# Feed-forwards fed with the unnormalised stream, and one convolution tile moved to TensorE, in a float32 four-layer model

## What is computed

```python
def rms_norm(x, g):
    y = x * lax.rsqrt(jnp.mean(x * x, axis=-1, keepdims=True) + EPS)
    return y * g
def swiglu(x, w_gate, w_up, w_down):
    return (jax.nn.silu(x @ w_gate) * (x @ w_up)) @ w_down

h = h + 0.5 * swiglu(rms_norm(h, ffn1_g), wg, wu, wd)     # 1024 -> 2816 -> 1024
h = h + mixer(rms_norm(h, mix_g))                         # even mixer in layer 0, odd mixer in layer 1
h = h + 0.5 * swiglu(rms_norm(h, ffn2_g), wg, wu, wd)
h = h + sigmoid(rms_norm(h, ple_g) @ wgate) * (p @ wproj)

def odd_mixer(xn):                                        # the second mixer
    u, v = split(gelu(xn @ w_in[:, :1024])); v = layer_norm(v)
    c_out = u * (w_s applied to v over blocks of 128 tokens, + c_b_s)
    a, g = split(xn @ w_in[:, 1024:]); hd = a * sigmoid(g)
    hd = causal depthwise convolution of hd, 31 taps, 512 channels, + d_conv_b
    d_out = silu(layer_norm(hd))
    return concat([c_out, d_out]) @ w_out
```

## Time and profile before

| | us |
|---|---|
| runs (3), median | 3446.67 (3442.4 to 3448.03) |
| the profiled execution, device time | 3462.87 |
| its span in the trace | 3461.6 |
| TensorE busy | 3215.9 (93% of the span), mean granted clock 0.95 |
| VectorE busy | 1208.5 (35%) |
| ScalarE busy | 1120.6 (32%) |
| GpSimd busy | 1203.7 (35%) |
| chain that ended last | PE 87%, DVE 8%, issue 1%, ACT 1%, POOL 1%, DMA 1% |

### The profile page before, as it was taken

One profiled execution on the slowest core, in us unless ns is written; L12 is line 12 of the kernel. 1 busy time (PEld: TensorE's weight loads), 2 busy tenths in 40 slices (PEclk: granted clock), 3 DMA queues, 4 the chain that ended last, 5 costly groups with the idle time before them and its releaser, 6 DMA issues.

```text
span 3461.6 us, 36877 instructions
## 1 busy us (share of the span) xinstructions
PE 3215.9 (93%) x14620; PEld 2574.8 (74%) x14620; DVE 1208.5 (35%) x2276; ACT 1120.6 (32%) x1942; POOL 1203.7 (35%) x522
## 2 busy tenths in 40 slices
PE   7999998989999989999839999989999989999998
PEld 5888667767888768887617888768758877877786
DVE  4001485742001430013972111254444233155442
ACT  3222333333223432223203222343222341345422
POOL 3444431014444434444404444443314532300043
PEclk9999998799999999999969999989999999979999
DMA  4333221002333223333202333323213325300032
GB/s 127 96 97 97 82 73 37 1 19 92 95 96 97 84 75 97 98 98 95 91 0 93 96 98 98 91 80 104 91 38 97 98 77 171 105 6 1 13 96 74
DMA packets 76526, 274.51 MB, mean 79 GB/s; under 512 B 8471, under 2 KB 9367, under 8 KB 75972
## 3 DMA queue, kind: packets, MB, share of 16 engines
q1 hardware_dynamic: 76356, 272.16, 25.2%
HBM read 269.98 MB, written 2.15 MB: 79 GB/s over the span
## 4 chain that ended last, share of the span: by engine, by line
PE 87%; DVE 8%; issue 1%; ACT 1%; POOL 1%; DMA 1%; SPq 0%; ACTq 0%; DVEq 0%; POOLq 0%
PE ps L463 24%; PE ps L465 23%; PE ps L464 23%; PE ps L1251 4%; PE ps L1238 4%; PE ps L1228 4%; DVE arena L1848 3%; DVE inv L596 1%; PE ps L2270 1%; DVE arena L642 1%; PE ps L591 1%; POOL arena L582 1%; PE ps L2134 1%; PE ps L1446 1%; ACT w_hi L427 1%
## 5 line engine op out<-in xcount | busy, mean ns | idle before, releaser
L448 POOL TENSOR_TENSOR w_lo<-ring,w_hi 128x1024 fp32r<-128x1024 f32 x473 | 1147.5, 2427 | 2195.2 <-ACT w_hi L427 2195.2
L463 PE MATMUL ps<-x_hi,w_hi 128*128 128x512 f32 x2376 | 945.6, 398 | 49.2 <-DVE x_lo L637 49.2
L464 PE MATMUL ps<-x_lo,w_hi 128*128 128x512 f32 x2376 | 932.3, 392 | 0.0
L465 PE MATMUL ps<-x_hi,w_lo 128*128 128x512 f32 x2376 | 932.2, 392 | 0.0
L427 ACT CAST w_hi<-ring 128x1024 fp32r<-128x1024 f32 x473 | 494.3, 1047 | 947.3 <-PE ps L465 945.5
L463 PEld LDWEIGHTS ps<-x_hi,w_hi 128*128 128x128 f32 x2376 | 451.5, 190 | 152.1 <-issue 59.5
L464 PEld LDWEIGHTS ps<-x_lo,w_hi 128*128 128x128 f32 x2376 | 451.6, 190 | 98.7 <-issue 5.3
L465 PEld LDWEIGHTS ps<-x_hi,w_lo 128*128 128x128 f32 x2376 | 450.7, 190 | 95.6
L463 PE MATMUL ps<-r_hi,w_hi 128*128 128x512 f32 x1088 | 425.7, 391 | 20.7 <-issue 20.7
L464 PE MATMUL ps<-r_lo,w_hi 128*128 128x512 f32 x1088 | 425.3, 391 | 0.0
L465 PE MATMUL ps<-r_hi,w_lo 128*128 128x512 f32 x1088 | 424.9, 391 | 0.0
(11 more groups left out here) (202 smaller groups left out, 2763.6 us busy)
## 6 DMA issues: line engine op xcount, KB each, us to landing
ring<-in_stream SPq DMA_DIRECT2D x473, 512.0 KB, 3.6
arena<-in_cmp_w SPq DMA_DIRECT2D x16, 512.0 KB, 4.6
arena<-frev SPq DMA_DIRECT2D x1, 3072.0 KB, 15.0
h<-in_x SPq DMA_DIRECT2D x4, 512.0 KB, 5.6
out<-arena SPq DMA_DIRECT2D x4, 512.0 KB
arena<-in_p SPq DMA_DIRECT2D x2, 512.0 KB
arena<-in_mem SPq DMA_DIRECT2D x1, 1024.0 KB
arena<-in_pool_recip SPq DMA_DIRECT2D x1, 1024.0 KB
```

The lines of the kernel that those rows point to most:

```text
L448: self.nc.gpsimd.tensor_tensor(self.w_lo[:, n % SPLIT, :], self.ring[:, n % RING, :], self.w_hi[:, n % SPLIT, :].bitcast(F32), ALU.subtrac ...
L463: nc.tensor.matmul(out, a[0], b[0], start=start, stop=False)
L464: nc.tensor.matmul(out, a[0], b[1], start=False, stop=False)
L465: return nc.tensor.matmul(out, a[1], b[0], start=False, stop=stop)
```

## The change

**Feed.** For all four feed-forwards `Normalise` is replaced by `Feed`. Its operands are h times gain, without the norm's factor: ACT rounds (`Feed.round`), DVE makes the rest in one instruction (`Feed.rest`), from `h` itself as soon as a tile of `h` is written. In `Rows` and in the ple's `dense_gated` these steps are woven into the evacuation of the last tiles. The sum of squares moves into the feed-forward: ACT squares (`squares`), DVE adds 7 times (`add`), TensorE sums once (`total`, behind the gate product of tile 1), ACT roots, DVE inverts. The factor is then multiplied in at evacuation: DVE scales the gate product to SBUF, DVE scales the up product to SBUF, ACT applies SiLU, DVE multiplies. So SiLU now waits for DVE. The norms ahead of the two mixers, of ple and of the second block stay.

**Start.** The DMAs are issued as vec, x0, slab 0, x1, slab 1, x2, x3, cst; the small tables become an `Aside` of the first feed-forward, and `Rotary` stands behind its tile 1.

**Second mixer.** Convolution tile 3 goes to TensorE as 31 matmuls with diagonal weights, which ACT makes during the evacuations; DVE gates that tile behind tile 1. The layer norm over the convolution is woven with the normalisation and mixing of v. The output product starts with tile 0, then 4 to 7, then 1 to 3.

```diff
+class Feed:
+    def round(self, act, c):
+        if self.written:
+            act.wait_ge(k.s["h_written"].handle, k.s["h_written"].at(c + 1))
+        k.nc.scalar.activation(k.x_hi[:, c, :], k.h[:, c, :], ACT.Copy,
+                               scale=k.v(self.gain, c)).then_inc(self.rounded.handle, 1)
+    def rest(self, dve, c):
+        dve.wait_ge(self.rounded.handle, self.rounded.at(c + 1))
+        k.nc.vector.scalar_tensor_tensor(k.x_lo[:, c, :], k.h[:, c, :], k.v(self.gain, c), k.x_hi[:, c, :].bitcast(F32),
+                                         ALU.mult, ALU.subtract).then_inc(self.ready.handle, 1)
...
 class Rows:
+        if self.feed:
+            k.high(act, self.first + self.n - 1 + SPLIT)
+            for c in range(KT):
+                self.feed.round(act, c)
...
             self.evacuate(m, k.ps[:, (self.bank + m) % 8, :]).then_inc(self.read.handle, 1)
+            if self.feed and m >= 1:
+                self.feed.rest(dve, m - 1)
...
 def ffn(...):
-            norm.first_two(pe, [k.slab(pe, first + j, P) for j in range(2)], (P, P), (part, done))
+            feed.first_two(pe, [k.slab(pe, first + j, P) for j in range(2)], (part, done))
...
-                        pe.wait_ge(read.handle, read.at(f - 2))
+                        pe.wait_ge(up_scaled.handle, up_scaled.at(f - 2))
...
+                    if f == 1 and j == 0:
+                        feed.total(pe, total_bank)
...
-            norm.act(act)
+            feed.squares(act)
+            k.high(act, first + 3 + SPLIT)
+            feed.sqrt(act, total_bank)
...
-                act.wait_ge(part.handle, part.at(f + 1))
-                nc.scalar.activation(hidden[:, f, :], k.ps[:, 2 * (f % 3), :], ACT.Silu).then_inc(gate.handle, 1)
+                act.wait_ge(gate_scaled.handle, gate_scaled.at(f + 1))
+                nc.scalar.activation(hidden[:, f, :], hidden[:, f, :], ACT.Silu).then_inc(gate.handle, 1)
                 k.high(act, first + 2 * f + 1 + SPLIT)
...
-            norm.dve(dve)
-            if rotary:
-                rotary.dve(dve)
+            feed.add(dve)
+            feed.invert(dve)
...
+                dve.wait_ge(part.handle, part.at(f + 1))
+                nc.vector.tensor_tensor(hidden[:, f, :], k.ps[:, 2 * (f % 3), :], inv, ALU.mult).then_inc(gate_scaled.handle, 1)
+                dve.wait_ge(done.handle, done.at(f + 1))
+                nc.vector.tensor_tensor(up[:, f % 2, :], k.ps[:, 2 * (f % 3) + 1, :], inv,
+                                        ALU.mult).then_inc(up_scaled.handle, 1)
...
+                nc.vector.tensor_tensor(hidden[:, f, :], hidden[:, f, :], up[:, f % 2, :], ALU.mult).then_inc(ready.handle, 1)
+                if rotary and f == 1:
+                    rotary.dve(dve)
...
 def odd_mixer(k):
+            for tap in range(31):
+                ins = nc.tensor.matmul(k.ps[:, conv_bank, :], diag[:, tap, :], g[:, last, tap:tap + SEQ],
+                                       start=(tap == 0), stop=(tap == 30))
```

More of the change, by code:

```diff
@@ L808, in dense_gated @@
     n = len(widths)
-    free = k.s["h_written"] if square else read
+    free = k.s["h_written"] if square or feed else read
     k.slabs_end(done, [done.at(m + 1) for m in range(n)])
@@ L866, in _ @@
                         rows.rest(dve, i)
+                if feed and m == n - 1:
+                    for c in range(2):
+                        feed.rest(dve, c)
                 dve.wait_ge(gate.handle, gate.at(m + 1))
                 ins = finish(m, buf[0:w, m % 4, :])
-                ins.then_inc((k.s["h_written"] if square else read).handle, 1)
+                ins.then_inc(free.handle, 1)
+            if feed:
+                for c in range(2, KT):
+                    feed.rest(dve, c)
             if square:
@@ L876, in dense_gated @@
             k.bank_read[m % 8] = gate.token(m + 1)
-    for g in (done, gate) + (() if square else (read,)):
+    for g in (done, gate) + (() if square else (free,)):
         g.advance(n)
@@ L952, in dve @@
             self.square.dve(dve)
-        else:
+        elif self.feed:
+            self.feed.rest(dve, KT - 1)
+        if not self.square:
             self.read.advance(KT)
@@ L1163, in _, with ple @@
             down.dve(dve, 5)
-    norm.close()
+    feed.close()
     if projection:
         projection.close()
-    for g in (part, done, gate, read):
+    for g in (part, done, gate, ready, gate_scaled, up_scaled):
         g.advance(FT)
-def ple(k, layer, projection):
+def ple(k, layer, projection, feed=None):
     nc = k.nc
@@ L1855, in last_tiles @@
[L1855 to L1865 removed]
+            gate(c)
@@ new lines, in _ @@
+            for c in range(4):
+                act.wait_ge(centred.handle, centred.at(c + 1))
+                nc.scalar.activation(sq[:, c, :], o[:, 4 + c, :], ACT.Square).then_inc(squared.handle, 1)
+            act.wait_ge(sums.handle, sums.at(4))
+            nc.scalar.activation(root, k.ps[:, square_bank, :], ACT.Sqrt, bias=k.c("eps"),
+                                 scale=1.0 / 512).then_inc(lrooted.handle, 1)
+            act.wait_ge(mix_done.handle, mix_done.at(1))
+            rows.round(act, 0)
@@ L1935, with tile_ready @@
+    def tile_ready(act, i):
+        if OD_ROWS[i] < 4:
+            act.wait_ge(mix_done.handle, mix_done.at(OD_ROWS[i] + 1))
+        else:
+            act.wait_ge(s["conv_silu"].handle, OD_ROWS[i] - 3)
+    rows.alone(tile_ready, begun=1)
+    mix_done.advance(4)
+    return feed
 MEM_KV = (10240, 8192)
```

413 lines of the change are left out of this document (278 added, 135 removed).

## The result

| | before | after |
|---|---|---|
| median of the runs, us | 3447.35 (3442.4 to 3455.49, 4 runs) | 3374.03 (3361.68 to 3375.78, 4 runs) |
| the profiled execution: time, span | 3462.87, 3461.6 | 3361.68, 3359.6 |
| TensorE busy | 3215.9 (93%) | 3188.5 (95%) |
| VectorE busy | 1208.5 (35%) | 1314.3 (39%) |

The ratio is 0.9771 (95% interval 0.975 to 0.9792), 73.3 us less. The forecast was 3373. Single executions are read here by stretches of their traces, not by their times: the runs come from several chips, and on one of them a run of before took 3455.32.

What follows compares the result with a forecast made beforehand. TensorE, busy 93%, was taken to bound the kernel, so gains come only where it stands still or runs slowly. Terms 11.8 + 11.5 + 10.6 + 3.9 + 35.8 = 73.6 us, off the median 3446.7: 3373.1; range 3359 to 3395.

Steps and rivals of the forecast that it cites:

- Second mixer: Last value matmul to output product: starts 34.5 us earlier, about 1.3 more from the slow clock; 35.8 gained.
- Odd handover: Layer 1, mixer to feed-forward: 14.2 us of gap and slow clock go, 2.4 lost again; 11.8 gained.
- Even handover: Layer 0, mixer to feed-forward: 13.9 us of gap and slow clock go, 2.4 lost again; 11.5 gained.
- ple: Handover from ple to feed-forward: a 4.6 us wait stays; 11.5 gained less 0.9 for the sum, 10.6.
- Start: First feed-forward: 13.8 us gained, less 0.9, 2.2 for other products, 4.8 waiting behind angle tables, 2.0 in clock; 3.9.
- rival 1: First feed-forward: no wait behind the angle tables, a further 6.8 us less, giving 3366; chance 0.15.
- The other tiles: Feed-forward tile loops: SiLU may be 7.1 us late, scaling makes it 1.3 late; costed at nothing.
- The rule against one term: Mixer handovers: DVE's two-operand instructions hold POOL too, delaying splits; each would gain 0.7 us less, sum 72.2.
- 2: Second mixer: TensorE keeps 1.2 GHz through the taps, which take 52.7 us; 3394; chance 0.08.
- 3: Handovers keep gaps of 3 to 6 us and the clock falls: 4 less each, 16 in all; 3389; chance 0.11.
- 4: Tile loops: DVE's chain makes TensorE wait once per tile, 88 times; at 1 us 3461; chance 0.03.
- 5: TensorE waits for a bank or ACT at each start, so only the mixer's tail gains; 3411; chance 0.03.

Runs made afterwards that it cites:

- mixer_only: The kernel before with only the new second (odd) mixer, feed-forwards still normalised by `Normalise`; 3419.13 us, ratio 0.9917.
- gate_early: The changed kernel with the gate of tile 3 ahead of tile 1's taps on DVE instead of behind them; 3378.28 us in one run.
- feed_only: The changed kernel with the old second mixer and plain output row order, still fed into the changed feed-forward; 3412.58 us, ratio 0.9896.
- after_again: The changed kernel run again unaltered, in more rounds; 3374.07 us, ratio 0.9786.
- rotary_split: The changed kernel with the angle tables' DVE work in two pieces, behind tiles 3 and 4, ACT's part behind tile 6; 3369.23 us, one run.
- loop_probe: The changed kernel with two more unused reciprocals per tile on DVE, from the fifth tile on, in all four feed-forwards; 3377.62 us, one run.
- rotary_tile9: The changed kernel with the angle tables whole but behind tile 9, ACT's part at tile 11; 3363.94 us, one run.
- best_taps8: The changed kernel with the three edits, the last tile's gate early and 8 of tile 2's taps moved to TensorE; 3364.36 us, ratio 0.9761.
- three edits: The changed kernel with angle tables in two pieces, tile 1 applied before the scalings, ACT's rounding before the cast at ple; together 3369.47 us, ratio 0.9773.
- ple_round_first: The changed kernel with ACT rounding the first two tiles behind ple before casting the next weight slab; 3361.74 us in one run.

## Why the prediction was right, point by point

- **Second mixer.** Predicted 34.5 + 1.3; measured 34.2 from the last value matmul to the output product, and 36.6 in the odd stretch of mixer_only. The waits came as written: about 8 for the gate (8.1) and 6 before the fourth group (5.7). The taps took 29.4 us where 30.5 were put down. The prediction said that TensorE's end lies under DVE's; gate_early shows it.
- **Odd handover.** Predicted 11.8, feed_only's odd stretch gives 12.7. **Even handover:** 11.5, measured 12.5 (after_again) to 13.1. The mechanism held, and the losses were set somewhat too high; against mixer_only's even stretch (440.4) the even gain is 11.4 to 12.0, so it is the rows that show this, not the stretches. TensorE runs through without a gap and at 1.00. DVE's rows there:

```profile
1777.34 1.97 DVE L585 SCALAR_TENSOR_TENSOR x_lo<-h,vec,x_hi 128x512 fp32r<-128x512 f32 x1
1779.23 0.68 DVE L2018 TENSOR_TENSOR h<-ps,h 128x512 f32<-128x512 f32 x1
1779.83 0.73 DVE L585 SCALAR_TENSOR_TENSOR x_lo<-h,vec,x_hi 128x512 fp32r<-128x512 f32 x1
1780.49 0.68 DVE L2018 TENSOR_TENSOR h<-ps,h 128x512 f32<-128x512 f32 x1
```

  The rest takes the 0.73 to 0.74 that the nearest row gave (0.75 taken), but the step is 1.26 us for a pair, not 1.43: one starts 0.1 us before the other's record ends. The seven pairs are 1.2 us sooner done, so the third slab's split isn't late (0.5 had been charged), and the sum waits 0.6 instead of 1. One rest is blocked by POOL, 1.97, as charged.
- **ple.** Predicted 10.6, measured 11.8 to 12.4. The wait is 4.39 where 4.6 was predicted, for the reason given: cast, rounding, POOL's split over the first rest. About 0.6 to 1.0 of the surplus lies ahead of TensorE's last ple product (54.9 and 55.3 us behind the landmark instead of 55.9), in code that is not changed.
- **Start.** Predicted 3.9, measured 4.3 and 4.7, against a start of before that is 393.9 (mixer_only, the same code) to 395.7: so 2 to 5. First slab at 14.87 (14.4 predicted), 13.3 gained instead of 13.8. The wait behind the tables is 4.13 (4.8), but the clock after it cost more than the 2.0: from 59.65 the slab took 8.34 us instead of 5.44, 2.9 lost. With these the sum gives 3.2; the 0.9 and 2.2 of the other products weren't measured alone. rotary_split measures wait and clock together, 7.0, where rival 1 had priced 6.8. The "9 matmuls" of the earlier trace rows take in those cut by the window's edges; they start every 0.427 us, the step that the sum used.
- **The other tiles.** Costed at nothing, with 7.1 us of slack as cover; loop_probe (6.7 us covered) and rotary_tile9 (11.5 us not) bound that cover from both sides.
- **The rule against one term.** It would have taken 0.7 per handover if DVE had held a split. At the odd handover none was: ACT's cast ends at 1776.28, and the split starts at 1776.35 at its usual length. But that doesn't speak against the rule, because DVE was then at an addition from PSUM (1775.85 to 1777.22), with one operand from SBUF. POOL's side of the lock shows in the rest of 1.97 us. The other side shows elsewhere in the same trace, in the split's length and not in its start: of the splits that stand alone, those that began while DVE did nothing took 2.34 to 2.41 us, those that began inside a DVE instruction with two SBUF operands up to 2.91, longer by what that instruction still had to run less some 0.14 us (last fence below: 0.59 left, 0.45 longer). Beside additions from PSUM they took 2.35 to 2.43. Of the splits behind the odd handover, three in a row from 1794.20 took 7.81 us beside DVE's sum of squares, against 7.01 for the three at 57.25, and TensorE didn't wait for them. The Trainium skill (SBUF — State Buffer, Who interferes with whom) has DVE hold POOL as well, and the trace agrees. The rule was sound; its 0.7 per handover fell away because no rest of DVE was running when a split began there.

```profile
1775.23 1.05 ACT L429 CAST w_hi<-ring 128x1024 fp32r<-128x1024 f32 x1 [3.92 <-PE ps L467]
```

```profile
1776.35 2.41 POOL L450 TENSOR_TENSOR w_lo<-ring,w_hi 128x1024 fp32r<-128x1024 f32 x1 [2.57 <-ACT w_hi L429]
```

```profile
2323.19 0.68 DVE L2284 TENSOR_TENSOR arena<-arena 64x504 f32<-64x504 f32 x1
...
2323.28 2.85 POOL L450 TENSOR_TENSOR w_lo<-ring,w_hi 128x1024 fp32r<-128x1024 f32 x1 [3.04 <-ACT w_hi L429]
```

- **TensorE's busy time.** Predicted to grow by some 27 us for the taps; it fell, from 3215.9 to 3188.5 (3204.7 in after_again). This sign was wrong. A matmul counts as busy for longer at the low clock, and the changed kernel's traces hold less of it: att 1 and att 2 alone are 24 us shorter in the first. mixer_only, which adds the taps and has a short att 2 (575.4), shows 3226.2, 10.3 more. So the busy time says nothing of added work where the clock differs.
- **The sum.** 73.6 predicted, 77.2 to 78.2 in the stretches that hold the change (after_again, after), 73.9 to 74.9 with mixer_only's start, even and ple in place of before's, 73.3 in the medians. So the terms were low by something between nothing and 4 us in all; one trace of before can't say more. The step from stretches to the time was the weak one: taking over the 16.2 by which the median lay below the profiled execution treated before's surplus as a constant of the trace. 13 of it is att 2, where before's profiled execution ran slowly (588.5), and such a surplus is an execution's, not a kernel's. The forecast came out because it was laid on the median, as it had to be. That it hit to 1 us is luck in part: its own bounds were 3361 to 3388, and an error of 2 to 4 us in the terms couldn't be told from the differences between executions.
- **Rivals.** 1 fell by the wait of 4.13; 2 by 29.4 us of taps (52.7 had it been so), though before's att 2 shows that the clock can stay at 0.50 for 40 us and more; 3 by handovers without gaps; 4 by loop_probe; 5 by feed_only.

## What to carry to other kernels

Where one engine is busy 95%, price a change at the places where it stands still, and name what is late next at each: each new wait came within 0.7 us of the size given. Deferring a factor to the evacuation takes the norm off the path but makes every step behind it late once, so move what is queued there (tables here) or cut it to less than the slack. An edit that removes a wait from an engine that isn't last gains nothing (gate_early) until the freed time is given work from the engine that is (best_taps8).

## What the runs showed that I had not expected

- The granted clock differed between executions of one program in stretches with many small gaps: 11 us in att 1 (331.9 and 342.9 for the same kernel), 13.3 in att 2 between kernels that are alike there.
- Gains of 2 to 4 us at one place were partly given back elsewhere at unchanged instructions (5.10 to 5.22 instead of 3.67 us for eight records; block 2 at 623.4 instead of 620.8), so three edits worth 12.8 us alone were worth 4.6 together.
- Short gaps that stand alone were cheap here: two of 1.8 and 2.0 us left the clock at 1.00, where behind one of 4.4 it was at 0.50 for about 5 us. Three of 0.3 to 1.24 us in a row ahead of the squares went with 0.50. Windows of ple_round_first across the first of them, and of the changed kernel behind its own:

```profile
1209.00:1211.00 2.00, 1.88 (x8) 1.61 (x9) 1.37 (x2) 2.00 (x4) 1.30 (x1) 1.00 0.01 4
1211.00:1214.00 3.00, 1.09 (x5) 0.56 (x3) 2.97 (x4) 2.77 (x5) 1.11 (x1) 1.00 0.26 38
```

```profile
1211.00:1214.00 3.00, 2.81 (x7) 2.26 (x8) 2.96 (x5) 2.78 (x5) 0.00 (x0) 0.50 0.59 175
```

- A table step that began just behind a split paid its whole length: the cast of positions took 2.62 us beside the split of 131.11 to 133.60 (rotary_tile9) and 0.42 without.

```profile
131.26 2.62 DVE L1506 CAST arena<-arena 128x512 f32<-128x512 int32 x1
```
